# Weight remainders held back until VectorE has normalised, and the predicated copy of a decay level put behind the scalings, in a two-layer decoder trunk

## The reference, cut to what matters

```python
def layer_norm(x, g, b):
    mu = jnp.mean(xf, axis=-1, keepdims=True)
    var = jnp.mean(jnp.square(xf - mu), axis=-1, keepdims=True)
    return (xf - mu) * lax.rsqrt(var + LN_EPS) * g + b

for l in range(2):
    h = swiglu(x, ffn_w1[l, 0], ffn_w3[l, 0], ffn_w2[l, 0])          # 1024 -> 2816 -> 1024
    x = layer_norm(ALPHA * x + 0.5 * h, ln_g[l, 0], ln_b[l, 0])
    h = hybrid_attention(x, ...) if l == 0 else hgrn2(x, ...)
    x = layer_norm(ALPHA * x + h, ln_g[l, 1], ln_b[l, 1])
    h = swiglu(x, ffn_w1[l, 1], ffn_w3[l, 1], ffn_w2[l, 1])
    x = layer_norm(ALPHA * x + 0.5 * h, ln_g[l, 2], ln_b[l, 2])
```

```python
b = jnp.cumsum(gc, axis=2)                       # log decays
diff = b[:, :, :, None, :] - b[:, :, None, :, :]
decay = jnp.exp(jnp.where(causal, diff, -jnp.inf))
a = jnp.einsum('bhtk,bhsk,bhtsk->bhts', qc, kc, decay)
o_intra = jnp.einsum('bhts,bhsv->bhtv', a, vc)
```

## Time and profile before

| | us |
|---|---|
| median of three runs | 2088.5 (2086.64 to 2088.7) |
| the profiled execution, whole | 2086.79 |
| its span on the core | 2085.1 |
| PE busy | 2032.4 (97%) |
| DVE busy | 736.2 (35%) |
| ACT busy | 552.5 (27%) |
| POOL busy | 907.2 (44%) |

### The profile page before, as it was taken

How to read it: one execution, slowest core, us unless ns; L and a number is a source line. 1 busy time by engine, 2 the same in 40 slices (tenths; PEclk the granted TensorE clock), 3 DMA queues, 4 the chain that set the end, 5 groups by cost and what they waited for, 6 DMA issues and landing times.

```text
span 2085.1 us, 26373 instructions
## 1 busy us (share of the span) xinstructions
PE 2032.4 (97%) x10521; PEld 1729.8 (83%) x10521; DVE 736.2 (35%) x1135; ACT 552.5 (27%) x654; POOL 907.2 (44%) x726
## 2 busy tenths in 40 slices
PE   8999999999999999999999999999999889999997
PEld 7888888988878888888888888888898878888886
DVE  3222222553365222223522222254543672222224
ACT  3222222343332222222322222232232123222221
POOL 4444444622215444444544444453443344444442
PEclk9999999999999999999999999999999999999999
DMA  5322322311103332222333233231211104323221
GB/s 205 103 97 101 101 84 98 107 61 52 51 20 122 101 101 91 92 99 81 122 101 97 84 101 101 81 122 47 75 61 61 55 7 162 97 84 101 101 80 41
DMA packets 135087, 184.75 MB, mean 89 GB/s; under 512 B 3168, under 2 KB 119024, under 8 KB 135024
## 3 DMA queue, kind: packets, MB, share of 16 engines
q1 hardware_dynamic: 134864, 183.59, 26.9%
q10 hardware_dynamic: 160, 0.26, 0.0%
HBM read 181.48 MB, written 2.10 MB: 88 GB/s over the span
## 4 chain that ended last, share of the span: by engine, by line
PE 92%; DVE 6%; issue 1%; ACT 0%; DMA 0%; POOL 0%; SPq 0%; DVEq 0%
PE psum L1064 28%; PE psum L1065 28%; PE psum L1066 28%; PE psum L1306 3%; PE psum L1251 2%; PE psum L1282 1%; DVE x L935 1%; DVE x L778 1%; DVE x L939 1%; PE psum L1266 1%; PE psum L1085 1%; DVE arena L875 0%; DVE xt_lo L759 0%; DVE arena L876 0%; DVE arena L866 0%
## 5 line engine op out<-in xcount | busy, mean ns | idle before, releaser
L519 POOL TENSOR_TENSOR w_lo<-raw,w_hi 128x512 fp32r<-128x512 f32 x652 | 852.7, 1339 | 1005.9 <-ACT w_hi L580 1005.9
L1064 PE MATMUL psum<-xt_hi,w_hi 128*128 128x512 f32 (+1 forms) x1824 | 678.7, 372 | 6.9 <-DVE xt_lo L759 6.6
L1065 PE MATMUL psum<-xt_lo,w_hi 128*128 128x512 f32 (+1 forms) x1824 | 673.9, 369 | 0.0
L1066 PE MATMUL psum<-xt_hi,w_lo 128*128 128x512 f32 (+1 forms) x1824 | 673.6, 369 | 0.0
L778 DVE SCALAR_TENSOR_TENSOR x<-psum,x 128x512 f32<-128x512 f32 x384 | 263.1, 690 | 577.8 <-PE psum L1066 577.4
L580 ACT ACTIVATE w_hi<-raw 128x2048 fp32r<-128x2048 f32 x165 | 315.0, 1909 | 381.3 <-PE psum L1066 380.6
L1064 PEld LDWEIGHTS psum<-xt_hi,w_hi 128*128 128x128 f32 x1824 | 346.9, 190 | 69.8 <-issue 10.6
L1066 PEld LDWEIGHTS psum<-xt_hi,w_lo 128*128 128x128 f32 x1824 | 346.7, 190 | 57.4
L1065 PEld LDWEIGHTS psum<-xt_lo,w_hi 128*128 128x128 f32 x1824 | 347.0, 190 | 55.8
L1064 PE MATMUL psum<-w_hi,h_hi 128*128 128x512 f32 x736 | 290.7, 395 | 3.9 <-DVE x L778 3.9
L1065 PE MATMUL psum<-w_lo,h_hi 128*128 128x512 f32 x736 | 289.7, 394 | 0.0
(11 more groups left out here) (113 smaller groups left out, 1229.1 us busy)
## 6 DMA issues: line engine op xcount, KB each, us to landing
raw<-in_ffn_w SPq DMA_DIRECT2D x132, 1024.0 KB, 5.3
raw<-in_hgrn_w_in SPq DMA_DIRECT2D x16, 1024.0 KB, 5.3
raw<-in_attn_w_in SPq DMA_DIRECT2D x9, 1024.0 KB, 5.2
raw<-in_attn_w_out SPq DMA_DIRECT2D x4, 1024.0 KB, 4.9
raw<-in_hgrn_w_out SPq DMA_DIRECT2D x4, 1024.0 KB, 5.0
lng<-in_ln_g SPq DMA_DIRECT2D x6, 512.0 KB, 5.0
lnb<-in_ln_b SPq DMA_DIRECT2D x6, 512.0 KB, 6.0
x<-in_x SPq DMA_DIRECT2D x4, 512.0 KB, 8.2
```

What stands on the lines that cost most here:

```text
L519: op = pool.tensor_tensor(w_lo[:, s % RING, cols], raw[:, s % RING, cols], w_hi[:, s % RING, cols].bitcast(F32), ALU.subtract)
L1064: pe.matmul(out_, w[0], xs[0], start=first, stop=False)
L1065: pe.matmul(out_, w[0], xs[1], start=False, stop=False)
L1066: return pe.matmul(out_, w[1], xs[0], start=False, stop=last)
```

## The change

There are two parts.

In POOL's program, three waits on `ln_done` are put ahead of remainders: at the end of an ffn the remainder of slab 2 waits until all four tiles are normalised; at the end of a mixer that of slab 1 waits for tiles 0 and 1, and that of slab 2 for all four.

In DVE's level, the predicated copy goes behind the three multiplies. It gets a semaphore of its own, `level_merged`: each copy waits for the one before it (both write into `within`), and PE's `updates`, which writes into the banks that the copies read, waits for all seven of its group. The unused `level_step` goes.

```diff
@@ gpsimd, end of an ffn
                     for j, tiles in enumerate(((0, 1), (2, 3), ())):
                         if n < last_phase:
+                            if j == 2:
+                                pool.wait_ge(ln_done, NT * (n + 1))
                             low(s0 + 3 * NG + j)
                         norm_powers(n, tiles)
@@ gpsimd, end of a mixer
                     for j, tiles in ((0, (0, 1)), (1, (2, 3)), (2, ())):
                         if j and n < last_phase:
+                            pool.wait_ge(ln_done, NT * n + 2 * j)
                             low(s0 + len(slabs) + j)
                         norm_powers(n, tiles)
@@ vector, level(g, a)
-                dst = at.rearrange("p (x b) e -> p x b e", b=64 // m)
-                dve.copy_predicated(dst, pair_mask[:, a - 1, :]...
-                                    bank[2 + a % 2].rearrange("p (x b e) -> p x b e", b=64 // m, e=m))
                 old = decay[:, par].rearrange("p h t -> p (h t)") if m == 1 else \
...
                 dve.tensor_tensor(block_decay[:, decay_at(2 * m):decay_at(2 * m) + 2 * n_], old[:, :, 0],
                                   old[:, :, 1], ALU.mult).then_inc(level_kept, 1)
+                dst = at.rearrange("p (x b) e -> p x b e", b=64 // m)
+                if 7 * g + a > 1:
+                    dve.wait_ge(level_merged, 7 * g + a - 1)
+                dve.copy_predicated(dst, pair_mask[:, a - 1, :]...
+                                    bank[2 + a % 2].rearrange("p (x b e) -> p x b e", b=64 // m, e=m)) \
+                    .then_inc(level_merged, 1)
                 dve.wait_ge(level_kept, 8 * g + a + 1)
@@ tensor, updates(g, blocks_needed)
+                pe.wait_ge(level_merged, 7 * g + 7)
                 pe.wait_ge(keys_tok_ready, 2 * g + 2)
```

More of the change, by code:

```diff
@@ L339, in build_trunk @@
         level_kept = sem("level_kept")
-        level_step = sem("level_step")
+        level_merged = sem("level_merged")
         gate_normed = sem("gate_normed")
@@ L863, in level @@
                 at = within[:].rearrange(pairs, two=2, e=m)[:, :, 1, :]
-                dst = at.rearrange("p (x b) e -> p x b e", b=64 // m)
-                dve.copy_predicated(dst, pair_mask[:, a - 1, :].rearrange("p (b e) -> p b e", e=m)[:, None, :, :]
-                                    .broadcast_to([P, 8, 64 // m, m]),
-                                    bank[2 + a % 2].rearrange("p (x b e) -> p x b e", b=64 // m, e=m))
                 old = decay[:, par].rearrange("p h t -> p (h t)") if m == 1 else \
@@ L877, in level @@
                                   old[:, :, 1], ALU.mult).then_inc(level_kept, 1)
+                dst = at.rearrange("p (x b) e -> p x b e", b=64 // m)
+                if 7 * g + a > 1:
+                    dve.wait_ge(level_merged, 7 * g + a - 1)
+                dve.copy_predicated(dst, pair_mask[:, a - 1, :].rearrange("p (b e) -> p b e", e=m)[:, None, :, :]
+                                    .broadcast_to([P, 8, 64 // m, m]),
+                                    bank[2 + a % 2].rearrange("p (x b e) -> p x b e", b=64 // m, e=m)) \
+                    .then_inc(level_merged, 1)
                 dve.wait_ge(level_kept, 8 * g + a + 1)
```

## The result

The changed kernel takes 2065.31 us (2064.58 to 2067.28, four runs), the kernel before 2087.61 in the same comparison (2086.64 to 2088.7, four runs): ratio 0.9895, 95% interval 0.9883 to 0.9907. That is 22.3 us faster.

A forecast was written before the change was run, and what follows sets the result against it. PE, busy 2032.4 of 2085.1 us, was taken as the bound, so only its waits or slow running matter. 7.94 (POOL's waits) + 4.0 (levels) + 1.0 (clock) = 12.9 us off 2087.7 gave 2075, range 2068.5 to 2081.5.

The forecast's parts named there:

- Part one, the sum: POOL's waits at the sub-layer ends: 2.30 at attention's, 1.90 at hgrn's, 3.74 at second and third ffn's, 7.94 us together.
- the two ffn ends: Second and third ffn's ends: tile 3's turn comes earlier, 1.87 us gained at the second, the third alike, 3.74 together.
- the nothing at the first: First ffn's end: PE already turned tiles 2 and 3 in one go, so gain 0.
- the cover of the later remainders: Delayed POOL remainders still ready before PE needs them, with 5 us to spare for slab 1 at attention's end; cost 0.
- Part two, the level term: hgrn's decay levels: PE's products wait for three instructions rather than four; 4.0 us taken, bounds 1.9 and 5.1.
- The plain sum: Copy lengths saved at four waiting level products: two of 0.63 and two of 1.12, 3.50 us.
- The clock term: Shorter PE waits win back 1 us lost to the lower TensorE clock, bounds -3 and +8.
- The 10.3 at stake: Estimated cost in us of five clock falls: 13.6 by depth times length, reduced for some 6.6 us of PE idle time.
- the clock comes back: Rival: with waits under 2 us the clock falls nearly all go, winning 8 us; 2068 us, chance 0.10.
- The waits did what they say: Against the rival that pairs stay near 4.4 us for another reason and only the levels count: 2084 us, chance 0.08.
- the levels gave: Against the rival that the levels give nothing and only POOL's waits count: 2080 us, chance 0.12.
- no more falls than before came: Against the slower rival, the clock falling at more of nine places: 2096 us, chance 0.03.

The follow-up runs named there:

- the copy behind alone: The kernel before with only the predicated copy moved behind the multiplies, without POOL's three waits: 2076.8 us, ratio 0.9951; run again, 2076.72 us.
- run with right-sized spare matmuls: The kernel before with 9, 13, 13 and 6 spare 64-column matmuls ahead of four level products that waited: 2081.83 us, ratio 0.9973.

## Why the prediction was wrong in size

- **Part one, the sum.** 7.94 was forecast. Between the milestones it gave 1.38 + 1.90 + 1.92 + 1.3 = 6.5, and alone 5.9 by the medians. The relief of 1.90 a pair, the two ffn ends, the nothing at the first, and the cover of the later remainders all held. What failed is a small step: I let the 1.9 us of an earlier restart pass through three groups at their old speed. The restart lies at the start of a fall, and more of PE's work now ran at the lower level (11.12 against 10.14 us). The prediction had tile 2's turn at 639.96; it came at 641.04.
- **Part two, the level term: the first failed step.** Taken 4.0, with an upper bound of 5.1; measured 5.9 of level waits (9.36 to 3.50) and 1.3 of waits for L778, whose additions stand behind a level on DVE and which the prediction did not have. I priced the removed copy by its own length and gave the start of one multiply, 0.82, to chance. On the trace the copy is the one instruction in the chain that the remainder does not slow (0.71 us at 1428.06 beside one, 0.76 at 1657.72 without), so in front it kept the multiplies waiting until POOL had begun; with it behind, two of the three start first. Three slowed multiplies in one level, not one, were the size to bound. One place gave nothing: at level 6 of the first pair POOL was busy with another two-input multiply before DVE began, and 2.15 stayed 2.14. The plain sum had 0.63 for it.
- **The clock term: the other failed step, and the larger.** Taken 1.0, within -3 and +8; measured 6.8 in hgrn, where three of the five falls of the earlier trace rows lay. The run with right-sized spare matmuls shows that idleness at the levels felled the clock and that this was worth 6.2 us by itself. The 10.3 at stake was read too low as well: the idle time that the prediction took off in the windows of hgrn lies ahead of the falls, and PE was busy all through them, so it is 6.8 there and about 11.5 in all (6.8, and half of the 5.1 and 4.4 us that PE was busy in the falls at the mixers' ends). The rival "the clock comes back" has this mechanism and 2068; I gave it 0.10 and put it in the wrong place: the mixers' falls, which it would have undone too, all stayed. The evidence against it was read too simply: I took the falls to stay because the waits would not vanish (2.9 to 1.8, 2.15 to 1.5 by the prediction). The wait of 2.15 stayed as it was and had no fall. That is in part luck. Only the fall behind the 2.88 went together with its wait; the other two, worth 5.1, had waits left behind which the copy behind alone still shows falls, and the changed kernel with spare matmuls at the mixers shows one of 3.4.
- **The sum of both misses.** 6.5 + 5.9 + 1.3 + 6.8 is 20.5 of the 20.9 us of span. The medians moved by 22.3; the 1.4 beyond the span is what the two profiled executions lie off their medians.
- **Rivals ruled out.** The waits did what they say (all pairs at 2.52); the levels gave; no more falls than before came. Of what I costed at nothing, no remainder and no `rstd` was late; the copies still cost some 1.4 us of waits ahead of L778's additions (2.6 with them, 1.2 without).

## What to carry to other kernels

Where a chain of two-input vector instructions races a two-input stream on GpSimdE, order decides twice: put first what that stream slows, and last what it doesn't. What such a meeting cost here was up to the length of the other engine's instruction, whatever the size of one's own. A wait of 1.4 to 3 us on TensorE is priced with the fall of the clock that may follow, about 1.7 or 3.4 us here, and the test is a run with spare matmuls sized by the trace, which takes away the fall and leaves the wait. The same wait can have a fall in one execution and none in another, so one profile doesn't show that a fall is gone for good: the mean granted clock of every execution tells more. When two edits give more together than apart, compare the granted clock of the two profiles before looking for a shared wait.

## What the runs showed of the hardware

- A DVE pair with two SBUF inputs, 128 x 1024 each, took 2.52 us alone, 3.10 beside a one-input copy on POOL, and 4.42 beside a two-input subtraction; POOL's four subtractions took 5.0 alone and 7.72 beside it. The two engines took turns by whole instructions: a DVE multiply of 32 elements a partition took 1.25 us, and ended with the subtraction (1431.75 to 1433.46) that it had met. DVE's instructions with one operand in PSUM, the predicated copy among them, kept their time.
- A float32 matmul with a 128 x 128 operand ran as two instructions of some 0.115 us, with 64 columns as with 128 (18 in 2.12 us, 32 in 3.73).
- The granted clock fell behind waits of 1.4 to 3.2 us in some executions and not behind the same waits in others; for the level waits of 2.1 and 1.4 us it went with where they lay on the even grid of the falls' starts. A wait of 1.8 us with ten matmuls ahead had no fall at attention's end in three profiles, where 1.25 and 2.58 us with a turn between had one of 0.57 over 8 us, and a short one (0.79 over 8 us) at hgrn's end.
